# Differential attention in two halves of four heads, woven with weight tiles

## The chip, the cores and the metric

The kernel runs on one core of a Trainium2 chip, as one program. The metric is its time on the device in microseconds (us), of whole executions.

## The reference

Three layers follow each other on a sequence of 256 tokens with 1024 channels: retention with a PEER feed-forward, differential attention with a PEER feed-forward, and a last block (SwiGLU, RWKV-7 beside forgetting attention, SwiGLU). Everything is float32. The change is in the second one's attention. `k_sh` and `v_sh` are products of that stage's input with `kv_w`, the keys rotated; there are 8 heads, each with two maps of 64 dimensions and a value of 128.

```python
def diff_attention(x, w_q, lam_p, subln_g, w_out, k_sh, v_sh, layer_idx, angles):
    q = (x @ w_q).reshape(b, s, DIFF_HEADS, 2, DIFF_HEAD_DIM)
    q = rope(q, angles) * (DIFF_HEAD_DIM ** -0.5)
    lam = jnp.exp(jnp.sum(lp[0] * lp[1])) - jnp.exp(jnp.sum(lp[2] * lp[3])) + lam_init
    for i in range(s // Q_BLOCK):                       # blocks of 128 queries
        sc = jnp.einsum('bqhmd,bkhmd->bhmqk', qb, kb)   # keys up to the block's end
        p = jax.nn.softmax(jnp.where(mask, sc, -jnp.inf), axis=-1)
        a = p[:, :, 0] - lam * p[:, :, 1]
        outs.append(jnp.einsum('bhqk,bkhe->bqhe', a, vb))
    o = o * lax.rsqrt(jnp.mean(jnp.square(o), axis=-1, keepdims=True) + LN_EPS)
    o = o * subln_g * (1.0 - lam_init)
    return o.reshape(b, s, DIFF_HEADS * DIFF_V_DIM) @ w_out
```

`rope` turns the first 16 of the 64 dimensions. A layer norm of the residual sum follows.

## The kernel before

**Weights.** All weight matrices are cut into tiles of 128x1024 float32 (512 KB). `weight_tiles` (L52) lists them in the order of use; SyncE loads them in that order into a ring of four buffers. A matmul is made of three: each tile is split into a rounded part `hi` (ScalarE, L859) and the remainder `lo` = tile - `hi`, by VectorE (L1226) where the list says "V", by GpSimd (L1828) where it says "P". Activations are split likewise, and the three products of the larger parts are summed in PSUM. There are three `hi` and three `lo` buffers. The function `split(i)` of each engine works through the list up to tile i and is called with the number of the tile in use + 2, so a tile's parts are made up to two tiles ahead; ScalarE's `hi` waits until TensorE has finished the tile three places back, VectorE's and GpSimd's `lo` waits for that `hi`. SyncE reloads a ring buffer once the `lo` part is done.

**Order.** Every engine runs a program of its own, written out in Python as a sequence of operations in order, with waits on counters of the other engines. Where several strands of work share an engine, each is a generator and `weave` (L374) takes one step of each in turn, in the same order on all engines; one turn over all strands is called a round here.

**Differential attention** (`diff` in all four programs; TensorE from L555, ScalarE from L969, VectorE from L1446). TensorE transposes the input (`parts`, L400), and computes q, k and v in six groups: two groups (columns 0 to 511 and 512 to 1023) for each of the three matrices, a group being four tiles and two PSUM banks (`mat_n`, L428, matmuls in L441 to L443). ScalarE copies each group into `D_nat` (L979). VectorE rotates q and k in 24 small operations after all projections, four times six; TensorE waits for the last and transposes both (32 transposes, L405), and VectorE and ScalarE copy the results.

Then four strands `heads(tt, h0)` are woven, one for each block of 128 queries (`tt`; 128 keys for tt = 0, "narrow", and 256 for tt = 1, "wide") and each half of the heads (h0 = 0 or 4). For each of its four heads a strand has two score matmuls, one after the other (L578, L581); VectorE's mask and maximum (in `softmax_in`, then a scale by -0.125); ScalarE's two exponentials with sums (L966); VectorE's combination of both maps (`diff_a`: reciprocal, times lambda, two multiply passes); TensorE's transpose (L589); ScalarE's copy of it (L995); the product with the values (L596). After four heads ScalarE copies the bank of outputs to `D_o` (L999). VectorE makes the sums of squares of all heads, GpSimd the power -1/2 (`power`, L1835), VectorE two multiplies for each block (by that, and by `subln_g` times a constant). TensorE transposes the result (16 transposes) and multiplies by `w_out` in eight tiles (`mat_out`, L449, L469 to L471), each of which adds into four PSUM banks. VectorE's layer norm closes the stage. All VectorE operations but `lo` go through one helper at L1203, the transposed splits of `parts` on ScalarE through L868 (or L871 with a gain).

PSUM has eight banks; `bank(..., among=...)` takes them in turn from a given set and waits until the former holder is emptied. In `diff` before, projections use all eight, the score and transpose tiles of a strand one bank, its outputs another.

Two things lie beside it on GpSimd's queue: the loads of the lambda and `subln_g` rows at the start, and the load of the next layer norm's gains (`gains`, after the last projection).

Of the kernel before, what the change touches and what calls it, by code (L numbers as in the profile page):

```python
# [21 lines left out]
LN_EPS = 1e-5  # L22
# [10 lines left out]
for _name, _w in (("ffn1", 8), ("mix", 8), ("ffn2", 8), ("mu", 14), ("w0", 4), ("a0", 4), ("kk", 4),  # L33
                  ("ka", 4), ("rk", 4), ("lg", 4), ("lb", 4), ("fb", 1)):
    COLS[_name] = _n
    _n += _w
# [15 lines left out]
def weight_tiles():  # L52
# [23 lines left out]
    for name in ("diff_q", "kv_k", "kv_v", "diff_out"):  # L76
        for i in range(8):
            add(name, i)
# [66 lines left out]
def program(nc, A, out):  # L145
    ctx = ExitStack()
    with ctx:
# [129 lines left out]
        D_lamt, D_lp, D_ls, D_sub = a_(256), a_(128), a_(8), a_(128)  # L277
        D_nat = [a_(2048).rearrange("p (a d) -> p a d", a=2) for _ in range(3)]
        D_r = [a_(128).rearrange("p (h d) -> p h d", h=16) for _ in range(4)]
# [4 lines left out]
        for tt in range(2):  # L284
            for h0 in (0, 4):
                D_hd[tt, h0] = (a_(512).rearrange("p (m k) -> p m k", m=2), a_(512).rearrange("p (m k) -> p m k", m=2),
                                a_(256), a_(256), a_(2), a_(4))
        D_rr = a_(16).rearrange("p (a h) -> p a h", a=2)
# [97 lines left out]
        def tensor_program(pe):  # L386
# [168 lines left out]
            def diff():  # L555
                pe.wait_ge(*at(dve, "norm", 0, 1))
                parts("diff", lambda tt, c: tok3(x, tt, c), 8)
                for z in range(3):
                    for nb in range(2):
                        for _ in mat_n([TILE[D_names[z], nb * 4 + j] for j in range(4)], "diff", "diff_p", z, nb,  # L560
                                       first=z + nb == 0):
                            pass
                pe.wait_ge(*at(dve, "diff_rope"))
                parts("diff_q", lambda tt, c: tok3(D_nat[0], tt, c), 8)
                parts("diff_k", lambda tt, c: tok3(D_nat[1], tt, c), 8)
                for z in ("diff_q", "diff_k"):
                    for c in (4, 6):
                        pe.wait_ge(*(at(dve, z, "Tn", c) if c == 4 else at(act, z, "Tn", c)))

                def heads(tt, h0):  # L570
                    s, p, a2, aT, mx, ss = D_hd[tt, h0]
                    own = (tt * 2 + h0 // 4,)
                    for _ in range(tt):
                        yield
                    kw = 128 * (tt + 1)
                    for h in range(h0, h0 + 4):
# [8 lines left out]
                        yield  # L585
# [6 lines left out]
                        if h == h0:  # L592
                            ob = bank("diff_o", tt, h0, among=(4 + tt * 2 + h0 // 4,))
                        pe.wait_ge(*at(act, "diff_aT", tt, h))
                        for kb in range(tt + 1):
                            ins = pe.matmul(ob[:, (h % 4) * 128:(h % 4) * 128 + 128], aT[:, kb * 128:kb * 128 + 128],  # L596
                                            D_nat[2][:, kb, h * 128:h * 128 + 128], start=kb == 0, stop=kb == tt)
                        mm.done(ins, "diff_av", tt, h)

                weave([heads(tt, h0) for tt in range(2) for h0 in (0, 4)])  # L600
                pe.wait_ge(*at(dve, "diff_norm"))
                parts("diff_oT", lambda tt, c: tok3(D_o, tt, c), 8)
                mat_out("diff_out", [TILE["diff_out", i] for i in range(8)], lambda k: D_oT[:, k, :],
                        lambda k: [at(dve, "diff_oT", "Tl", k)] if k % 2 == 0 else [])
# [239 lines left out]
        def scalar_program(a):  # L844
# [18 lines left out]
            def parts(stage, nchunk, dst, gain=None):  # L863
                for c in range(0, nchunk, 2):
# [1253 lines left out]
```

## Time and profile before

| | us |
|---|---|
| median of three runs | 3005.3 (3004.41 to 3005.68) |
| the profiled execution | 3003.82 |
| its span, first to last instruction | 3001.8 |
| TensorE matmul busy | 2782.4 (93%) |
| VectorE busy | 1894.4 (63%) |
| ScalarE busy | 1239.1 (41%) |
| GpSimd busy | 770.4 (26%) |
| mean granted TensorE clock | 0.949 |

The profile is of one execution; its span leaves out 2.0 us around the first and last instruction. Engines are named PE (TensorE matmuls), PEld (its weight loads), DVE (VectorE), ACT (ScalarE), POOL (GpSimd). The tiles of this stage lie in one large area, so most of them appear under the name W. A float32 matmul of the heads appears as two records, a transpose as one. PEclk is the share of 2.4 GHz that TensorE was granted: 1.00 is 2.4 GHz, 0.50 is 1.2 GHz, and a value between them is a mixture in time. In a timeline, times are from the span's start, and a bracket says how long the engine was idle before and on whom it waited.

### The profile page before, as it was taken

The numbers are of one execution on the slowest core, as the hardware profiler recorded it, in microseconds if no ns is written. First come the engines' busy times: TensorE is split into PE (matmuls) and PEld (weight loads), VectorE is DVE, ScalarE is ACT, GpSimd is POOL, SyncE is SP. The second block draws the span as 40 slices with busy tenths as digits, with TensorE's granted clock in tenths as the row PEclk, the third lists the DMA queues.
The fourth block names the chain that finished last, engine by engine and source line by source line (L and its number), as shares of the span: only waits on it lengthen the run. The fifth ranks groups of instructions, "written<-read, shape, count | busy, mean of one in ns | idle before, by whom it ended". The sixth has DMA issues, their size and how long they took to land.

```text
span 3001.8 us, 43611 instructions
## 1 busy us (share of the span) xinstructions
PE 2782.4 (93%) x17592; PEld 2512.5 (84%) x17592; DVE 1894.4 (63%) x3246; ACT 1239.1 (41%) x1691; POOL 770.4 (26%) x336
## 2 busy tenths in 40 slices
PE   8989999999999988699999999999799858898998
PEld 7869999998888866499999988888798746776896
DVE  5655997776555556659977765555654675415554
ACT  4434463333545434244633345445444512132443
POOL 0001986664000000019876630000000230042000
PEclk9999999999999997699999999999899878889999
DMA  5454554445656643145544456656455410023554
GB/s 203 162 176 155 175 181 144 141 141 163 193 192 190 192 153 106 57 155 174 178 155 141 141 169 190 193 192 190 135 183 192 127 59 23 1 84 99 157 184 144
DMA packets 122919, 449.55 MB, mean 150 GB/s; under 512 B 13728, under 2 KB 13856, under 8 KB 122592
## 3 DMA queue, kind: packets, MB, share of 16 engines
q1 hardware_dynamic: 120800, 439.47, 45.9%
q0 software_dynamic: 1920, 7.30, 0.8%
q8 instruction: 140, 2.29, 0.3%
q14 instruction: 59, 0.48, 0.1%
HBM read 445.67 MB, written 1.05 MB: 149 GB/s over the span
## 4 chain that ended last, share of the span: by engine, by line
PE 84%; DVE 12%; ACT 2%; POOL 2%; issue 1%; DMA 0%; DVEq 0%; SPq 0%; ACTq 0%
PE ps L419 11%; PE ps L420 11%; PE ps L421 11%; PE ps L471 10%; PE ps L470 10%; PE ps L469 10%; DVE W L1203 9%; PE ps L538 4%; PE ps L623 3%; PE ps L441 2%; PE ps L442 2%; PE ps L443 2%; DVE x L1203 1%; PE ps L405 1%; POOL lo L1828 1%
## 5 line engine op out<-in xcount | busy, mean ns | idle before, releaser
L859 ACT ACTIVATE hi<-ring 128x1024 fp32r<-128x1024 f32 x830 | 878.5, 1059 | 1273.8 <-PE ps L421 649.8
L1226 DVE TENSOR_TENSOR lo<-ring,hi 128x1024 fp32r<-128x1024 f32 x544 | 665.7, 1225 | 604.2 <-ACT hi L859 604.0
L419 PE MATMUL ps<-xT_r,hi 128*128 128x256 f32 x3248 | 935.5, 288 | 11.7 <-POOL lo L1828 8.1
L420 PE MATMUL ps<-xT_r,hi 128*128 128x256 f32 x3248 | 921.1, 284 | 0.0
L421 PE MATMUL ps<-xT_r,lo 128*128 128x256 f32 x3248 | 920.8, 283 | 0.0
L1828 POOL TENSOR_TENSOR lo<-ring,hi 128x1024 fp32r<-128x1024 f32 x286 | 724.3, 2540 | 595.5 <-ACT hi L859 595.5
L419 PEld LDWEIGHTS ps<-xT_r,hi 128*128 128x128 f32 x3248 | 625.2, 192 | 15.6 <-POOL lo L1828 5.5
L420 PEld LDWEIGHTS ps<-xT_r,hi 128*128 128x128 f32 x3248 | 625.8, 193 | 0.7 <-issue 0.7
L421 PEld LDWEIGHTS ps<-xT_r,lo 128*128 128x128 f32 x3248 | 625.2, 192 | 0.0
L469 PE MATMUL ps<-hi,oht_r 128*128 128x512 f32 x1040 | 405.6, 390 | 13.6 <-DVE W L1203 13.6
L471 PE MATMUL ps<-hi,oht_r 128*128 128x512 f32 x1040 | 411.3, 395 | 0.0
L470 PE MATMUL ps<-lo,oht_r 128*128 128x512 f32 x1040 | 409.2, 393 | 0.0
L1835 POOL TENSOR_TENSOR small<-small,con 128x2 f32<-128x2 f32 (+2 forms) x16 | 16.3, 1018 | 1103.6 <-DVE small L1203 1103.6
L1203 DVE TENSOR_TENSOR W<-W,ps 128x512 f32<-128x512 f32 x240 | 164.6, 686 | 204.3 <-PE ps L538 119.5
L469 PEld LDWEIGHTS ps<-hi,oht_r 128*128 128x128 f32 x1040 | 196.2, 189 | 57.9 <-DVE W L1203 14.0
L470 PEld LDWEIGHTS ps<-lo,oht_r 128*128 128x128 f32 x1040 | 196.2, 189 | 45.9
L471 PEld LDWEIGHTS ps<-hi,oht_r 128*128 128x128 f32 x1040 | 196.4, 189 | 39.3
L1400 DVE TENSOR_SCALAR oht<-ps,selT 128x128 f32<-128x128 f32 x512 | 174.2, 404 | 0.0
L441 PE MATMUL ps<-hi,xT_r 128*128 128x512 f32 x336 | 138.9, 413 | 9.6 <-POOL lo L1828 6.0
L1203 DVE TENSOR_TENSOR W<-W 128x512 f32<-128x512 f32 (+6 forms) x127 | 128.1, 1009 | 16.4 <-ACT W L1043 7.5
L538 PE MATMUL ps<-oht 128*128 128x128 f32 x1024 | 134.6, 274 | 0.0
L442 PE MATMUL ps<-lo,xT_r 128*128 128x512 f32 x336 | 134.0, 399 | 0.0
(212 smaller groups left out, 2906.1 us busy)
## 6 DMA issues: line engine op xcount, KB each, us to landing
ring<-in_peer_u SPq DMA_DIRECT2D x256, 512.0 KB, 3.5
ring<-in_peer_v SPq DMA_DIRECT2D x256, 512.0 KB, 3.4
ring<-in_f SPq DMA_DIRECT2D x132, 512.0 KB, 3.6
ring<-in_ret_vg SPq DMA_DIRECT2D x32, 512.0 KB, 3.5
ring<-in_peer_q SPq DMA_DIRECT2D x32, 512.0 KB, 3.6
ring<-in_ret_qk SPq DMA_DIRECT2D x16, 512.0 KB, 3.8
ring<-in_ret_out SPq DMA_DIRECT2D x16, 512.0 KB, 4.1
ring<-in_in_shift SPq DMA_DIRECT2D x14, 512.0 KB, 4.1
```

The costliest lines, as they stand in the source:

```text
L419: pe.matmul(o, h, xT[:, k, 0:256], start=k == 0, stop=False)
L420: pe.matmul(o, h, xT[:, k, 256:512], start=False, stop=False)
L421: ins = pe.matmul(o, l, xT[:, k, 0:256], start=False, stop=k == 7)
L441: pe.matmul(bs[tt], xh, h, start=kk == 0, stop=False)
L469: pe.matmul(b, ah, h, start=k == 0, stop=False)
L470: pe.matmul(b, ah, l, start=False, stop=False)
L471: ins = pe.matmul(b, al, h, start=False, stop=k == len(tiles) - 1)
L538: ins = pe.matmul(b[:, s * 128:s * 128 + 128], hot[:, s, 1, :], hot[:, s, 0, :], start=True, stop=True)
L859: hid.done(a.activation(hi[m % NH][:, :], ring[j % NR][:, :], ACT.Copy), j)
L1203: dve.done(fn(*args), *name)
L1226: lo_v.done(v.tensor_tensor(lo[m % NH][:, :], ring[j % NR][:, :], as32(hi[m % NH][:, :]), ALU.subtract), j)
L1828: lo_p.done(p.tensor_tensor(lo[m % NH][:, :], ring[j % NR][:, :], as32(hi[m % NH][:, :]), ALU.subtract), j)
```

## The change

It rewrites `diff` in the four programs.

- **Halves.** All work goes in two halves of four heads (`nb` = 0, 1). The weight list takes the q, k and v tiles of heads 0 to 3 first, then those of heads 4 to 7. Of the second half's q and k tiles the odd ones are given to GpSimd ("P") for the `lo` part.
- **Rotation** is done per matrix and half (`rope(z, nb)`, six operations on both blocks at once), each called among the splits of later tiles.
- **First weave.** After three groups (12 tiles) and the transposes of q and k of heads 0 to 3, the heads of half 0 are woven with the 8 tiles of q and k of half 1: a strand `tiles_b`, first in the order, with one tile in each round, and four strands `heads(0, tt, u)` of two heads each, which start 0, 1, 1 and 2 rounds late. A head takes three rounds: scores (mask, maximum, exponentials), combination and transpose, product and output.
- **Between** come two value tiles and the transposes of q and k of half 1.
- **Second weave.** The heads of half 1 are woven with `tiles_c`: the norm of half 0 (VectorE only), two value tiles, the transposes of half 0's output, and four tiles of the output product.
- **After it** come the norm and transposes of half 1 (inside `mat_out_steps`, ahead of tile 4) and the last four output tiles.
- **Norm.** For every head and block ScalarE copies the 128x128 output and also squares it with a sum (`Square`, `accum_out`), so VectorE's squares and sums go; the sums of each half get their own power on GpSimd, and VectorE multiplies once per block by power and constant. `subln_g` becomes a column of per-partition gains applied in the two parts of the transposed output (`parts` with a gain), instead of a loaded row and a multiply.
- **Banks.** Projections and output product use banks 4 to 7; each strand's scores, transposes and outputs share one bank of 0 to 3.

The diff, cut to its core (`parts` and `natural` get an argument `first`; gains are passed as a function; ScalarE's `heads` follows the same steps):

```diff
-    for name in ("diff_q", "kv_k", "kv_v", "diff_out"):
-        for i in range(8):
-            add(name, i)
+    for half in range(2):
+        for name in ("diff_q", "kv_k", "kv_v"):
+            for i in range(half * 4, half * 4 + 4):
+                add(name, i, "P" if half and i % 2 and name != "kv_v" else "V")
+    for i in range(8):
+        add("diff_out", i)
...
+                def heads(nb, tt, u):          (TensorE)
+                    own = (tt * 2 + u,)
+                    for _ in range(tt + u):
+                        yield
...
+                    for h in range(nb * 4 + u * 2, nb * 4 + u * 2 + 2):
                         b = bank("diff_s", tt, h, among=own)
...
                         mm.done(ins, "diff_s", tt, h)
                         yield
-                        yield
                         b = bank("diff_t", tt, h, among=own)
                         pe.wait_ge(*at(dve, "diff_a", tt, h))
...
                         yield
+                        ob = bank("diff_o", tt, h, among=own)
                         pe.wait_ge(*at(act, "diff_aT", tt, h))
...
+                        yield
+                def out_ahead(k):
+                    if k == 4:
+                        pe.wait_ge(*at(dve, "diff_norm", 1))
+                        parts("diff_oT", lambda tt, c: tok3(D_o, tt, c), 8, among=LO4, first=4)
+                for z in range(3):
+                    for _ in group(z, 0):
+                        pass
+                turned(0, 0)
+                turned(1, 0)
+                def tiles_b():
+                    for z in range(2):
+                        yield from group(z, 1)
+                        yield
+                weave([tiles_b()] + [heads(0, tt, u) for u in range(2) for tt in range(2)])
+                values = group(2, 1)
+                next(values)
+                turned(0, 1)
+                next(values)
+                turned(1, 1)
+                output = mat_out_steps("diff_out", ..., among=HI4, ahead=out_ahead)
+                def tiles_c():
+                    yield from values
+                    yield
+                    pe.wait_ge(*at(dve, "diff_norm", 0))
+                    parts("diff_oT", lambda tt, c: tok3(D_o, tt, c), 4, among=HI4)
+                    yield
+                    for _ in range(4):
+                        next(output)
+                        yield
+                weave([tiles_c()] + [heads(1, tt, u) for u in range(2) for tt in range(2)])
+                for _ in output:
+                    pass
...
+                def group(z, nb):              (ScalarE)
+                    for j in range(4):
+                        split(TILE[D_names[z], nb * 4 + j] + 2)
+                        if j < 3:
+                            yield
+                    for tt in range(2):
+                        a.wait_ge(*at(mm, "diff_p", z, nb))
...
+                        a.wait_ge(*at(mm, "diff_av", tt, h))
+                        o = ps("diff_o", tt, h)[:, 0:128]
+                        act.done(a.activation(D_o[:, tt, h * 128:h * 128 + 128], o, ACT.Copy))
+                        act.done(a.activation(D_sq[...], o, ACT.Square, accum_out=D_rr[nb][...]), "diff_o", nb)
+                        empties(act, "diff_o", tt, h)
+                        yield
...
+                def rope(z, nb):               (VectorE)
+                    v.wait_ge(*at(act, "diff_p", z, nb, 1))
+                    tt_(r[0], x1, dcos, ALU.mult)
...
+                def norm(nb):
+                    v.wait_ge(*at(act, "diff_o", nb))
+                    rsqrt(D_rr[nb], D_rr[nb], 1.0 / 128, LN_EPS, "diff", nb)
+                    for tt in range(2):
+                        stt_(ov, ov, 1.0 - LAM_INIT, b3(D_rr[nb][...], [128, 4, 128], 2), ALU.mult, ALU.mult, name=("diff_norm", nb))
+                def tiles_b():
+                    for z in range(2):
+                        for j in range(4):
+                            tiles(z, 1, (j,))
+                            if z == 1 and j == 1:
+                                rope(0, 1)
+                            yield
...
+                tiles(2, 1, (0,))
+                rope(1, 1)
+                tiles(2, 1, (1,))
+                natural("diff_q", 8, D_qT, first=4)
+                natural("diff_k", 8, D_kT, first=4)
+                def tiles_c():
+                    norm(0)
+                    for j in range(2, 4):
+                        tiles(2, 1, (j,))
+                        yield
+                    parts("diff_oT", 4, D_oT, lambda c: pc("dsub"))
+                    yield
+                    for i in range(4):
+                        split(TILE["diff_out", i] + 2)
+                        yield
...
-            load("diff", [(D_lamt, prow(12, 256)), (D_sub, prow(11, 128))], [at(dve, "norm", 0, 1)])
+            load("diff", [(D_lamt, prow(11, 256))], [at(dve, "norm", 0, 1)])
+            split(TILE["kv_k", 7])             (GpSimd)
+            power(D_rr[0], "diff", 0)
             gains(1, 0, mm, "diff_p", 2, 1)
-            power(D_rr, "diff")
+            power(D_rr[1], "diff", 1)
```

## Rows read from the trace of the kernel before

**Rows 1.** The page's chain that ended last, by engine

```profile
PE 84%; DVE 12%; ACT 2%; POOL 2%; issue 1%; DMA 0%; DVEq 0%; SPq 0%; ACTq 0%
```

**Rows 2.** Windows of the differential-attention stage (first line: columns)

```profile
core 0: us, PE busy (x) PEld busy (x) DVE busy (x) ACT busy (x) POOL busy (x), PEclk, DMA share, GB/s
1092.50:1155.10 62.60, 62.60 (x276) 51.77 (x276) 30.18 (x29) 31.12 (x36) 0.00 (x0) 1.00 0.58 182
1155.10:1165.50 10.40, 2.94 (x14) 2.09 (x13) 8.15 (x25) 2.15 (x3) 1.06 (x2) 0.79 0.68 219
1165.50:1172.70 7.20, 6.53 (x32) 6.29 (x32) 2.77 (x4) 2.39 (x4) 0.00 (x0) 0.60 0.01 2
1172.70:1227.20 54.50, 48.75 (x136) 28.95 (x136) 39.93 (x114) 21.31 (x84) 0.00 (x0) 0.52 0.00 1
1227.20:1238.70 11.50, 0.04 (x1) 0.04 (x1) 7.56 (x8) 0.58 (x1) 2.93 (x1) 0.50 0.00 0
1238.70:1242.30 3.60, 3.60 (x17) 3.60 (x18) 1.53 (x3) 1.79 (x3) 0.00 (x0) 0.50 0.00 0
1242.30:1264.70 22.40, 22.40 (x97) 17.98 (x95) 11.04 (x10) 8.95 (x9) 0.00 (x0) 0.98 0.53 164
```

**Rows 3.** Timeline 1155 to 1173: start us, length us, engine, line, operation

```profile
1155.40 1.06 ACT L859 ACTIVATE hi<-ring 128x1024 fp32r<-128x1024 f32 x1 [1.66 <-PE ps L443]
...
1156.50 1.23 DVE L1226 TENSOR_TENSOR lo<-ring,hi 128x1024 fp32r<-128x1024 f32 x1 [1.49 <-ACT hi L859]
...
1165.48 6.54 PE L405 MATMUL ps<-con,W 128*128 128x128 f32 x32 [7.46 <-DVE W L1203]
...
1172.92 0.46 PE L578 MATMUL ps<-W 64*128 64x128 f32 x2 [0.89 <-ACT W L877]
```

**Rows 4.** Timeline of the heads, 1180 to 1192, blocks of 256 keys

```profile
1180.32 0.51 ACT L966 ACTIVATE W<-W 128x256 f32<-128x256 f32 x1 [0.85 <-DVE W L1203]
...
1181.23 0.18 ACT L966 ACTIVATION_READ_ACCUMULATOR W<-W 128x1 f32 x1
...
1183.48 0.17 DVE L1203 RECIPROCAL W<-W 128x2 f32<-128x2 f32 x1
...
1183.87 0.36 DVE L1203 TENSOR_SCALAR W<-W 128x256 f32<-128x256 f32 x1
...
1184.26 0.48 DVE L1203 SCALAR_TENSOR_TENSOR W<-W 128x256 f32<-128x256 f32 x1
...
1184.90 0.66 PE L589 MATMUL ps<-con,W 128*128 128x128 f32 x2 [0.71 <-DVE W L1203]
...
1191.19 1.22 PE L581 MATMUL ps<-W 64*128 64x256 f32 x2
```

**Rows 5.** Groups by form, heads: count | busy us, mean ns | idle

```profile
L1203 DVE TENSOR_TENSOR W<-ps,con 128x512 f32<-128x512 f32 x8 | 5.5, 692 | 5.4 <-PE ps L581 4.8
...
L1203 DVE TENSOR_TENSOR W<-ps,con 128x256 f32<-128x256 f32 x8 | 3.4, 425 | 2.4 <-PE ps L578 1.6
```

**Rows 6.** Timeline of the mixer, 2465 to 2475

```profile
2465.93 0.69 DVE L1203 TENSOR_TENSOR W<-W,small 128x512 f32<-128x512 f32 x1 [1.75 <-POOL small L1835]
...
2471.62 5.11 POOL L1828 TENSOR_TENSOR lo<-ring,hi 128x1024 fp32r<-128x1024 f32 x2
2471.69 2.81 DVE L1203 TENSOR_TENSOR W<-W,small 128x512 f32<-128x512 f32 x1 [1.75 <-POOL small L1835]
...
2474.02 0.79 PE L441 MATMUL ps<-hi,xT_r 128*128 128x512 f32 x1 [4.50 <-POOL lo L1828]
...
2474.61 0.63 PE L442 MATMUL ps<-lo,xT_r 128*128 128x512 f32 x1
```

**Rows 7.** Groups by form, whole run

```profile
L1203 DVE SCALAR_TENSOR_TENSOR xT_r<-ps,col,xT_r 128x256 fp32r<-128x256 f32 x24 | 11.6, 484 | 7.6 <-ACT xT_r L871 6.2
...
L884 ACT ACTIVATE W<-x 128x512 f32<-128x512 f32 x16 | 10.1, 630 | 24.3 <-DVE x L1203 24.1
...
L1835 POOL TENSOR_TENSOR small<-small,con 128x8 f32<-128x8 f32 x4 | 6.6, 1653 | 31.3 <-DVE small L1203 31.3
```

More of the change, by code:

```diff
@@ new lines, in diff @@
+                weave([tiles_b()] + [heads(0, tt, u) for u in range(2) for tt in range(2)])
[4 more added lines that the diff above has]
+                turned(1, 1)
+                output = mat_out_steps("diff_out", [TILE["diff_out", i] for i in range(8)], lambda k: D_oT[:, k, :],
+                                       lambda k: [at(dve, "diff_oT", "Tl", k)] if k % 2 == 0 else [], among=HI4, ahead=out_ahead)
@@ L860, in split, with parts @@
                     todo[0] += 1
-            def parts(stage, nchunk, dst, gain=None):
-                for c in range(0, nchunk, 2):
+            def parts(stage, nchunk, dst, gain=None, first=0):
+                for c in range(first, nchunk, 2):
                     pv = j2(ps(stage, "T", c))
@@ L870, in parts, with natural @@
                         for j in range(2):
-                            act.done(a.activation(dst[:, c + j, 0:256], pv[:, j, :], ACT.Identity, scale=pc(gain, c + j)),
+                            act.done(a.activation(dst[:, c + j, 0:256], pv[:, j, :], ACT.Identity, scale=gain(c + j)),
                                      stage, "Th", c)
-            def natural(stage, nchunk, dst):
-                for c in range(2, nchunk, 4):
+            def natural(stage, nchunk, dst, first=0):
+                for c in range(first + 2, nchunk, 4):
                     a.wait_ge(*at(mm, stage, "T", c))
@@ L1227, in split, with parts @@
                     todo[0] += 1
-            def parts(stage, nchunk, dst, gain=None):
-                for c in range(0, nchunk, 2):
+            def parts(stage, nchunk, dst, gain=None, first=0):
+                for c in range(first, nchunk, 2):
                     pv = j2(ps(stage, "T", c))
@@ L1512, in diff @@
+                weave([tiles_c()] + [heads(1, tt, u) for u in range(2) for tt in range(2)])
+                norm(1)
+                parts("diff_oT", 8, D_oT, lambda c: pc("dsub"), first=4)
+                for i in range(4, 8):
                     split(TILE["diff_out", i] + 2)
@@ L1543, in mixer @@
                 rms("mix", M_xs)
-                parts("mix", 8, xT, "mix")
+                parts("mix", 8, xT, lambda c: pc("mix", c))
                 for i in range(2):
```

202 lines of the change are left out of this document (100 added, 102 removed).

## The prediction

> **What bounds the kernel now.** I read the chain of waits first: TensorE holds 84% of it and VectorE 12% [rows 1]. A change pays where TensorE stands still or runs slowly, so next I cut the differential-attention stage at TensorE's own stops and asked for busy time and granted clock by stretch [rows 2]. From the first projection matmul (1092.5) to the last one of the output product (1264.7) it takes 172.2 us. Six projection groups: 24 tiles in 62.6 us, 2.61 us a tile, TensorE always busy, clock 1.00. Rotation: 10.4 us, of which 7.5 us idle [rows 2, 3]. Transposes of q and k: 7.2 us. Heads: 54.5 us, TensorE busy 48.7 us of them, but at 0.52: almost all at the 1.2 GHz level. Norm and its transposes: 11.5 + 3.6 us. Output: 22.4 us. The DMA share is 0.58 at most while tiles run, so loads bound nothing here.
>
> **The change, part by part.** All other stages keep their instructions. The sum is a new length for the 172.2 us.
>
> *First three groups.* 12 tiles x 2.61 = 31.3 us. Rotation of q and k now runs in VectorE's slack under later tiles. Work for one tile is a `hi` part of 1.06 us and a `lo` part of 1.23 us [rows 3], begun two tiles (5.2 us) before use, so 2.9 us are free; one rotation is six operations of 0.3 us, 1.9 us (a quarter of the 24 in the 7.9 us before the transposes). Hidden: 0. Were this cover gone, each of the four would cost 1.9 us.
>
> *Transposes of the first half of q and k.* 16, where 32 took 6.6 us [rows 3]: 3.3 us at the low clock, half of it at the high one. I take 2.7. The copies behind them lie under the first woven tile.
>
> *The two weaves.* This decides. Engines work in order, and in each round of a weave every engine's tile step stands ahead of its four head steps. ScalarE cannot begin the next `hi` before the last exponential of the round; VectorE cannot take the next head step before `lo`, which waits for that `hi`; TensorE waits for VectorE's combination `diff_a` before it transposes, and its next scores stand behind that transpose. So a round is a loop through three engines, not the busiest engine's sum. Its links, for a wide head (256 keys): combination 1.25 us (from the reciprocal's start at 1183.48 to 1184.74); exponentials 1.1 (0.51 to the end of the second read, 1180.32 to 1181.41); score pair 2 x 1.22 = 2.4 at the low clock [rows 4], 1.2 at the high one, since the narrow pair began there at 0.46 [rows 3]; mask and maximum 0.69 each, scale 0.17 (as the reciprocal's), with gaps 1.6 [rows 4, 5]. Narrow (128 keys), from 0.43 for the mask [rows 5] and scaled likewise: 1.1, 0.9, 1.0, 1.05. Transpose with its hops 0.45 to 0.6; copy of the transposed block 0.4; output copy plus squares 0.6.
> Rounds 2 and 5 (transpose, transpose, wide score): 1.1 + 1.25 + 1.25 + 1.1 + 0.45 + 1.2 + 1.6 + 1.1 = 9.05. Rounds 1 and 4 (a narrow transpose, then both scores): 1.1 + 1.25 + 1.1 + 0.45 + 1.2 + 1.6 + 1.05 + 0.9 = 8.65. Round 3: 1.1 + 1.25 + 1.05 + 2.1 (an exponential, two outputs) + 0.4 = 5.9. Round 6: 1.1 + 1.25 + 1.25 + 0.6 = 4.2. Where GpSimd makes the `lo` part (rounds 1, 3 and 5 of the first weave), `hi` and `lo` leave the loop: minus 2.35; in round 3 TensorE's tile and score then hold it, plus 0.8; round 5 carries a rotation, plus 1.9.
> First weave: start 5.6 (tile, score, mask, exponential) + 6.3 + 9.05 + 4.35 + 8.65 + 8.6 + 4.2 + last round 3.2 = 50.0 us. Second: start 7.9, for the first half's norm sits ahead of the mask (0.2 + 1.65 for the power [rows 7] + 2 x 0.75), + 8.65 + 8.9 (output transposes' two parts, 2.2, in place of `hi` and `lo`) + 5.9 + 8.65 + 9.05 + 4.2 + 1.0 = 54.3 us.
>
> *Clock in the weaves.* Before, the heads never left the low level though TensorE was 90% busy [rows 2]. Here a round has one tile and stops of up to 5 us. After a stop of 4.50 us the mixer's tile restarts with two matmuls 0.59 us apart, where twelve share 2.61 us [rows 6]: the low level. A slow tile is mostly hidden in the loop's wait; slow scores are not. All low: four wide scores a weave x 1.2, plus the tile ahead of round 3's score, 13 us in both. All high: 0. Between ends this far apart I take the middle, 6.5, since a round is half dense tile and half short work.
>
> *GpSimd's four tiles.* In the mixer a 128x512 VectorE operation with both inputs in SBUF took 0.69 us alone and 2.81 us when it began just behind a GpSimd split [rows 6]: 2.1 us lost. Four splits: 0 to 8.4 us; two of them fall on combinations, so I take 3. The Trainium skill (SBUF — State Buffer, "Who interferes with whom") has the rule: a VectorE instruction with two SBUF inputs contends with a GpSimd instruction that reads SBUF, and the loser waits for the whole instruction. It speaks against this part; by it every split would lose its 2.1 us to some operation of VectorE and the sum be 5.4 us longer, 177.9; the trace agrees that the loss is the rest of the split.
>
> *Between the weaves.* Two tiles and 16 transposes, 5.2 + 2.0 = 7.2 us; the last rotation ends 6 us into it and is just hidden.
>
> *Tail.* Output copy and squares 0.8, scale 0.2, power 1.65, two multiplies 1.4, four transposes 0.9 (3.6 for 16), their two parts 1.7 (VectorE's 0.48 a chunk [rows 7], ScalarE's about the same, overlapped): 6.7 us, where 15.1 stood. Then four output tiles, 10.8 us.
>
> *Edits at nothing.* ScalarE's squares: a 128x512 one is 0.63 us [rows 7], the 128-wide one lies between 0.2 and 0.6; 16 of them are in the rounds above, and cost up to 0.3 us each if ScalarE ends the loop. Gain per chunk in the transposed copies: same count of stages, two instructions for one, 0.4 us in all. The load of the gain row goes from GpSimd's queue, which was idle. In that queue the four splits and the first half's power now stand ahead of the next norm's gains, needed only at the layer norm, 12 tiles later. SyncE's order of loads changes, not its number: a slot is reloaded when its `lo` is done, and at the 182 GB/s of the projections [rows 2] a tile of 512 KB comes in 2.9 us, less than any round.
>
> Sum: 31.3 + 2.7 + 50.0 + 7.2 + 54.3 + 6.7 + 10.8 = 163.0, plus 3 (port), plus 6.5 (clock) = 172.5 us against 172.2. The profiled execution took 3003.8 us (span 3001.8 and 2.0 around it), 1.5 below the median 3005.3; a difference carries over, so I forecast 3005.5. Ends: 163.0 gives 2996, 163.0 + 13 + 8.4 = 184.4 gives 3017.5. Said otherwise: the gaps give 21 us (rotation 10.4, transposes 2.5, tail 8.4) and the weaves give it back: with port and clock 114 us, for heads and 14 tiles that took 54.5 + 36.7.
>
> **Rivals.** *A, the engines run ahead of each other.* The weaves then cost TensorE's own work: 14 tiles 36.7, transposes 1, heads 48.7 us halved by the clock with some left over, 27; 65 us, with today's stretch (54.5/48.7) 72. Stage 131, time 2964. For it: neither ScalarE nor VectorE has much over 30 us of work in a weave by the links above (VectorE's heads 4 x (1.6 + 1.25 + 1.05 + 1.1) = 20, `lo` parts 5 to 7.4, rotation or norm 2). Against: the order of steps above, which leaves each only one round of slack. Halfway, 2984.
>
> *B, slower by the clock.* Stops of 4 to 5 us in rounds 2 and 5 drop TensorE to 1.2 GHz for most of both weaves; scores double and a tile of 5.1 us no longer fits under rounds 3 and 6. It decides once over two thirds of the weaves run low: the other 6.5 us of the clock term give 3012, and some 2.3 us for the tile in each of four rounds 3021. For it: the stretch from 1172.7 on; against: rounds of 4 us without a long stop.
>
> *C, the rotation is not hidden* (a barrier elsewhere): up to 7.6 us back, inside the range. The change cannot fail to act: the order of all five streams is written out.
>
> **How the numbers follow.** About 0.2% (6 us) is what a measurement of this kernel can tell from no change. The loop with mixed clock: 0.52, 2996 to 3017.5, of which faster 0.12, same 0.27, slower 0.13. A or part of it: 0.24, faster. B: 0.22, slower. C: 0.02, same. Faster 0.36, same 0.29, slower 0.35. The range takes A's half-way point and most of B: 2982 to 3021.
>
> **What would show it.** Right: no TensorE stop before the transposes of q and k; weaves of 50 to 60 us each with waits of TensorE on VectorE of 3 to 5 us before the head transposes, and of `lo` on `hi` on exponentials; clock there 0.6 to 0.9; a tail of 6 to 8 us; DMA idle. Wrong: weaves of 35 to 40 us (A), clock near 0.50 in them (B), or VectorE's combinations unchanged beside GpSimd's splits (no port term).

## The result, and the profile after

| | before | changed |
|---|---|---|
| median of 16 runs, us | 3004.8 (3002.8 to 3010.1) | 3013.4 (3010.9 to 3018.5) |
| span of the profiled execution, us | 3001.8 | 3011.6 |
| from the first projection matmul to the last of the output product, us | 172.2 | 179.2 |
| mean granted TensorE clock | 0.949 | 0.953 |

The changed kernel takes 1.0028 times the time of before, 95% interval 1.0020 to 1.0036: 8.4 us slower, a little more than the 6 us that were called the limit of no change. Of the 9.8 us between the two spans 7.0 lie in this stage, 0.9 before it and 1.9 behind it.

The windows of the changed kernel's stage, in the columns of [rows 2] (length; busy us and count of PE, PEld, DVE, ACT, POOL; PEclk; DMA share; GB/s). In order: first three groups, first transposes of q and k, first weave, between, second weave, tail, last four output tiles.

```profile
1093.40:1127.30 33.90, 33.90 (x146) 27.90 (x146) 18.68 (x29) 16.64 (x19) 1.50 (x1) 0.97 0.54 169
1127.30:1129.00 1.70, 1.70 (x17) 1.70 (x16) 1.07 (x2) 1.58 (x3) 0.88 (x1) 1.00 0.09 34
1129.00:1186.40 57.40, 45.38 (x166) 31.67 (x165) 28.57 (x68) 23.23 (x73) 7.05 (x3) 0.79 0.23 74
1186.40:1193.70 7.30, 7.30 (x42) 6.19 (x41) 4.81 (x10) 3.61 (x8) 0.00 (x0) 1.00 0.46 144
1193.70:1252.75 59.05, 40.87 (x148) 27.68 (x147) 29.66 (x70) 22.28 (x74) 2.81 (x3) 0.77 0.25 80
1252.75:1259.96 7.21, 1.97 (x10) 1.60 (x9) 2.57 (x6) 2.54 (x8) 1.66 (x1) 0.74 0.00 1
1259.96:1272.60 12.64, 12.64 (x48) 9.97 (x48) 5.73 (x6) 3.79 (x4) 0.00 (x0) 0.88 0.39 126
```

The stop before the transposes of q and k is gone, and the tail is 7.2 us where [rows 2] has 11.5 + 3.6. The time came back in the two weaves: 57.4 and 59.1 us, in which no engine is full. VectorE is busy for half of them, ScalarE for 40%, and TensorE stands still for 12 us of the first and 18 us of the second. Round 2 of the first weave shows why; this is its timeline (start us, length us, engine, line, operation, idle before and releaser):

```profile
1141.26 0.19 ACT L1005 ACTIVATION_READ_ACCUMULATOR W<-W 128x1 f32 x1
1141.35 1.04 ACT L898 ACTIVATE hi<-ring 128x1024 fp32r<-128x1024 f32 x1
...
1142.43 1.23 DVE L1294 TENSOR_TENSOR lo<-ring,hi 128x1024 fp32r<-128x1024 f32 x1 [1.89 <-ACT hi L898]
...
1143.57 0.16 DVE L1271 RECIPROCAL W<-W 128x2 f32<-128x2 f32 x1
...
1143.96 0.35 DVE L1271 TENSOR_SCALAR W<-W 128x256 f32<-128x256 f32 x1
1144.35 0.48 DVE L1271 SCALAR_TENSOR_TENSOR W<-W 128x256 f32<-128x256 f32 x1
...
1144.97 0.66 PE L594 MATMUL ps<-con,W 128*128 128x128 f32 x2 [3.52 <-DVE W L1271]
```

The last exponential's sum is read; only then comes `hi`, only then `lo`, only then the combination, and TensorE has stood still for 3.5 us. The chain of waits goes through such a `hi` behind the exponentials five times in the two weaves (at 1141.4, 1179.1, 1200.8, 1237.0 and 1247.5). Behind the stops it goes through a score pair and then through TensorE's tile at the low clock: the tile from 1149.0 to 1154.2 took 5.2 us. The waits of both weaves (1129 to 1253; engine, line, whom it waited for: us in total, times, longest):

```profile
ACT W L1005 <- DVE W L1271: 38.6, 12, 4.7
...
PE ps L594 <- DVE W L1271: 28.6, 15, 5.0
DVE W L1271 <- PE ps L587: 26.2, 11, 4.5
ACT W L1032 <- PE ps L594: 24.5, 16, 3.5
...
DVE lo L1294 <- ACT hi L898: 22.5, 11, 2.7
```

Exponentials wait for the maximum, transposes for the combination, masks for the scores, copies for the transposes: a ring of waits.

### The profile page after: what moved, and what is told of

It reads as the page before. It is cut to its first block, busy times and chain, and to the rows that moved or that the text cites. A ratio compares the mean times of both kernels' runs of the same rounds, so it can differ in the third digit from the quotient of the medians.

```text
span 3011.6 us, 43694 instructions
## 1 busy us (share of the span) xinstructions
PE 2782.8 (92%) x17592; PEld 2511.7 (83%) x17592; DVE 1884.4 (63%) x3243; ACT 1244.5 (41%) x1739; POOL 778.7 (26%) x340
## 4 chain that ended last, share of the span: by engine, by line
PE 82%; DVE 13%; ACT 2%; POOL 2%; issue 1%; DMA 0%; DVEq 0%; SPq 0%; ACTq 0%
PE ps L423 11%; PE ps L424 11%; PE ps L425 11%; PE ps L473 10%; PE ps L475 10%; PE ps L474 10%; DVE W L1271 10%; PE ps L542 4%; PE ps L662 3%; PE ps L445 2%; PE ps L446 2%; PE ps L447 2%; DVE x L1271 1%; POOL lo L1929 1%; PE ps L409 1%
## 5 line engine op out<-in xcount | busy, mean ns | idle before, releaser
L1929 POOL TENSOR_TENSOR lo<-ring,hi 128x1024 fp32r<-128x1024 f32 x290 | 732.8, 2534 | 669.8 <-ACT hi L898 669.8
L445 PE MATMUL ps<-hi,xT_r 128*128 128x512 f32 x336 | 142.5, 424 | 9.2 <-POOL lo L1929 5.5
L447 PE MATMUL ps<-hi,xT_r 128*128 128x512 f32 x336 | 136.3, 406 | 0.0
```

Source lines behind the costliest of these rows:

```text
L445: pe.matmul(bs[tt], xh, h, start=kk == 0, stop=False)
L1929: lo_p.done(p.tensor_tensor(lo[m % NH][:, :], ring[j % NR][:, :], as32(hi[m % NH][:, :]), ALU.subtract), j)
```

## The experiments

Each run has its own runs of the kernel before on the same chip; microseconds of a difference between two experiments are taken from their ratios, times 3004. By the intervals of the ratios such a difference is known to 4 to 5 us either way.

The whole time also holds the other stages, which no edit touches, and they did not always take the same time. So the length of this stage in each run's profiled execution is given beside it, as "stage": from the end of the input's transposes to the last matmul of the output product, 172.2 us before and 179.2 changed. What lies behind the stage took 1737.1 us before and 1739.0 in the changed kernel, but only 1730.3, 1729.8 and 1730.2 in three of the runs below (`lo` behind the head steps, the fourth corner, and the same head order inside the weaves). More than half of that difference lies in one stretch of the last block, from the `hi` of one weight tile to that of the next. Here it is in the changed kernel and then in these three:

```profile
2489.20:2653.60 164.40, 137.14 (x781) 119.04 (x780) 72.78 (x123) 35.22 (x79) 2.40 (x1) 0.79 0.02 7
2470.20:2629.40 159.20, 131.27 (x780) 113.59 (x779) 73.61 (x124) 35.12 (x78) 2.55 (x1) 0.82 0.02 8
2471.10:2630.10 159.00, 131.81 (x780) 113.99 (x779) 73.65 (x124) 35.09 (x78) 2.67 (x1) 0.81 0.03 8
2455.30:2614.50 159.20, 131.27 (x780) 113.61 (x779) 73.55 (x124) 35.12 (x78) 2.55 (x1) 0.82 0.02 7
```

The same matmuls were busy for 131 to 132 us instead of 137, at a granted clock of 0.81 or 0.82 instead of 0.79. It is not the chip: two other runs on the chip of the first of the three, those without GpSimd and with the rotation alone, took 1738.8 and 1737.5 us behind the stage. The reason is not shown. So up to 9 us of the gain of these three runs did not come about in this stage.

**VectorE's `lo` behind the head steps.** In VectorE's program alone:

```diff
-                weave([tiles_b()] + [heads(0, tt, u) for u in range(2) for tt in range(2)])
+                weave([heads(0, tt, u) for u in range(2) for tt in range(2)] + [tiles_b()])
...
-                weave([tiles_c()] + [heads(1, tt, u) for u in range(2) for tt in range(2)])
+                weave([norm_c()] + [heads(1, tt, u) for u in range(2) for tt in range(2)] + [tiles_c()])
```

`norm_c` holds the norm of half 0 and the parts of its transposes, in their old rounds.

> The changed kernel with one edit: in both weaves VectorE takes its tile step (the lo part) after the four head steps of a round instead of ahead of them; the half's norm and the parts of the output transposes stay first. The same instructions on every engine. Loop theory: in the eight rounds in which VectorE makes a lo part, lo (1.23 us) and the wait for hi (1.1 us) leave the chain from exponential to combination: 14 to 19 us less than the changed kernel, 2994 to 2999 us, so also 6 to 11 below the kernel before; each weave 47 to 52 us instead of 57.4 and 59.1. Rival (the weaves are long because TensorE's clock is low and its own work is slow): less than 4 us gained, 3009 to 3013.

Measured: 2990.3 us, ratio 0.9958 (0.9944 to 0.9972). That is 0.0070, or 21 us, below the changed kernel, and 13 us below the kernel before. Not one instruction was added or taken away. The stage took 164.1 us, 15.1 less than in the changed kernel, which is within the 14 to 19 us that the loop theory asked for; 8.7 of the 24 us between the two profiled executions lie behind the stage. Its weaves:

```profile
1128.70:1179.10 50.40, 41.41 (x168) 29.56 (x167) 29.60 (x68) 23.05 (x74) 7.06 (x3) 0.90 0.27 83
1186.10:1236.30 50.20, 36.98 (x151) 25.53 (x149) 29.53 (x71) 22.08 (x74) 2.81 (x3) 0.86 0.27 85
```

16 us come out of the weaves (57.4 + 59.1 to 50.4 + 50.2). TensorE stands still for 22 us of them instead of 30, and the clock is 0.90 and 0.86. How much of the gain is the clock's is not shown.

**GpSimd's four tiles given back to VectorE.**

```diff
-                add(name, i, "P" if half and i % 2 and name != "kv_v" else "V")
+                add(name, i)
```

> The changed kernel with the four tiles that GpSimd splits given back to VectorE. Loop theory: lo and the wait for hi come back into the chain of three rounds of the first weave, plus 7 us, less the one operation that the trace shows held by GpSimd (2.25 us where 0.35 is usual, minus 1.9): 3 to 6 us slower than the changed kernel, 3016 to 3019. Rival (the shared port is what makes the first weave long, 2.1 us for each tile): 3 to 8 us faster, 3005 to 3010.

Measured: 3018.2 us, ratio 1.0055 (1.0041 to 1.0068), 8 us slower than the changed kernel; stage 184.5, 5.3 longer. The rival is out: handing tiles to GpSimd helps here, as the loop theory says, by taking `lo` out of VectorE's order.

**No weave of tiles with heads.**

```diff
-                weave([tiles_b()] + [heads(0, tt, u) for u in range(2) for tt in range(2)])
+                weave([tiles_b()])
+                weave([heads(0, tt, u) for u in range(2) for tt in range(2)])
```

and so for the second, on all three engines.

> The changed kernel with its two weaves undone: on every engine the tile strand runs to its end and then the four head strands are woven with each other. Halves, rotation per half, ScalarE's squares and the short tail stay. Loop theory (the weave costs more than it covers): first stretch 8 tiles 21.8 + heads 27 + 3 to start and drain = 52 instead of 57.4, second 16.4 + 3 + 27 + 3 = 49 instead of 59.1: 12 to 18 us faster than the changed kernel, 2995 to 3001. Rival (the weave does cover tiles with heads, and the loss is elsewhere, in halves or squares): 0 to 20 us slower, 3013 to 3033.

Measured: 3015.3 us, ratio 1.0042 (1.0029 to 1.0056). A miss: undoing the weave gained nothing. By the whole time it cost 4 us, no more than the intervals allow for chance; the stage took 187.0 us, 7.8 more than in the changed kernel. A half of the heads alone takes 38.5 us and not 27 + 3:

```profile
1150.00:1188.50 38.50, 23.12 (x70) 13.65 (x70) 18.75 (x56) 14.55 (x63) 0.00 (x0) 0.57 0.06 21
1221.50:1260.30 38.80, 23.09 (x69) 13.39 (x68) 18.76 (x56) 13.47 (x62) 0.00 (x0) 0.57 0.05 14
```

TensorE is busy for only 23 of the 38.5 us, where [rows 2] has 48.7 of 54.5 for all eight heads. The price of the heads had been taken from an order that the changed kernel no longer has.

**The rotation alone.** Kernel before; in VectorE's loop over the tiles:

```diff
                         for j in range(4):
                             split(TILE[D_names[z], nb * 4 + j] + 2)
+                            if z and nb == 0 and j % 2:
+                                rope(z - 1, j // 2)
```

> The kernel before with one edit: each of the four rotations (a matrix and a block of 128 queries) is called among the splits of later tiles, after every second tile of the group that follows, instead of after all projections. Theory: TensorE's stop of 7.5 us before the transposes of q and k goes and nothing else moves: 2997 to 2998. Rival (a rotation of 1.9 us makes lo parts late and TensorE waits): 3000 to 3005.

Measured: 2995.3 us, ratio 0.9971 (0.9960 to 0.9981), 8.7 us faster; stage 161.9, 10.3 shorter. The stop of 7.5 us between the last tile and the transposes is gone and no tile is late: the 24 tiles took 65.5 us at clock 1.00. The transposes follow them at once at clock 1.00 and took 3.6 us, where [rows 2] has 7.2 us at 0.60.

**Filler matmuls, for the clock.** Changed kernel; the extra matmuls change no result:

```diff
                         b = bank("diff_t", tt, h, among=own)
+                        if tt == 1 and u == 0:
+                            for k in range(8):
+                                pe.matmul(b, xT[:, 4, 0:128], xT[:, 4 + k % 4, :], start=True, stop=True)
                         pe.wait_ge(*at(dve, "diff_a", tt, h))
```

> The changed kernel with eight dense 128x512 matmuls of no use (their bank is overwritten by the transpose that follows) ahead of TensorE's wait for the combination of the first wide strand, where the trace shows stops of 3.5 to 5.4 us: four places. Nothing is left out of the computation. Theory that the low clock costs some microseconds of the weaves: granted clock of the rounds around these stops goes from 0.64 to 0.70 up to over 0.9, the wide score pair behind each from 2.5 to 1.3 us and the tile behind it from 4.6 to 2.9, partly hidden: 4 to 8 us faster than the changed kernel, 3005 to 3009. Rival (the loop through VectorE and ScalarE hides TensorE's clock): 3012 to 3015.

Measured: 3006.5 us, ratio 1.0009 (1.0000 to 1.0017): 5.7 us below the changed kernel, by 32 matmuls of no use. Windows of the changed kernel (score pair behind the stop of round 2, then its tile), and of both weaves with filler:

```profile
1146.10:1149.02 2.92, 2.81 (x6) 1.25 (x6) 0.00 (x0) 0.28 (x1) 0.00 (x0) 0.50 0.08 32
1149.02:1153.60 4.58, 4.58 (x12) 3.61 (x12) 1.55 (x3) 2.04 (x5) 0.78 (x1) 0.50 0.00 0
```

```profile
1128.80:1185.40 56.60, 48.38 (x184) 34.55 (x182) 28.80 (x68) 23.28 (x74) 7.07 (x3) 0.85 0.24 75
1192.40:1251.80 59.40, 46.10 (x167) 31.90 (x164) 29.78 (x71) 22.17 (x74) 2.81 (x3) 0.80 0.24 80
```

The clock rises only from 0.79 and 0.77 to 0.85 and 0.80. Behind the first stop the first of the two wide score products took 0.7 us instead of 1.2, but the tile behind them took 5.5 us (1148.3 to 1153.8) where it had taken 5.2, and 2.9 had been expected. The two weaves took 116.0 us instead of 116.5 and the stage 178.7 instead of 179.2. The profiled execution, 3013.3 us, was the slowest of eleven (from 3003.8), so it may not be the typical one. So what the low clock cost in the weaves is not settled: the medians say 5.7 us (give or take 3.5), the trace shows 0.5.

**The parts of the transposes later,** on top of the first experiment: behind the head steps on VectorE, one round later on ScalarE, output tiles one round later.

```diff
                     for j in range(2, 4):
                         tiles(2, 1, (j,))
                         yield
+                    parts("diff_oT", 4, D_oT, lambda c: pc("dsub"))
+                    yield
                     yield
```

> The kernel of the run e1_lo_last with one edit in the second weave: both parts of the four output transposes come after the head steps of their round on VectorE and at the head of the next round on ScalarE, and the output tiles begin one round later, so that the last of them lies beside the last strand. Theory: the stop of 6.4 us that this round still has shrinks to 2 to 3 us: 3 to 5 us faster than e1_lo_last, 2985 to 2988. Rival (it only moves the wait to the first output tile): 2989 to 2992.

Measured: 2994.3 us, ratio 0.9963 (0.9950 to 0.9976), not to be told from 0.9958; stage 164.8 against 164.1. The rival held: the stop of 6.4 us became one of 2.9 and one of 6.0 before the next transposes, because VectorE's parts now stood ahead of the next combination and waited for ScalarE.

**Four strands of four heads, with the new norm.** The rotation run plus ScalarE's copy and square for each head, power for each block, one multiply, gain in the parts. No halves, no weave with tiles.

```diff
+                        a.wait_ge(*at(mm, "diff_av", tt, h))
+                        o = ps("diff_o", tt, h)[:, 0:128]
+                        act.done(a.activation(D_o[:, tt, h * 128:h * 128 + 128], o, ACT.Copy))
+                        act.done(a.activation(D_sq[...], o, ACT.Square, accum_out=D_rr[tt][:, h:h + 1]), "diff_o", tt)
```

> The kernel of the run e4_rotation_only (four strands of four heads, no halves, no weave with tiles) with the norm of the changed kernel: ScalarE copies and squares each head's output, GpSimd's power per block of queries, one multiply, gain in the parts of the transposes. Theory: VectorE's squares and one of two multiplies leave the stop of 11.5 us before the output transposes, minus 5 us; the 16 squares lie in ScalarE's idle time: 2989 to 2992. Rival (ScalarE's extra 0.6 us a head delays the exponentials of the next): 2995 to 3000.

Measured: 2989.1 us, ratio 0.9948 (0.9935 to 0.9961): 7 us below the rotation run; stage 154.5, 7.4 shorter. The squares cost next to nothing here, where ScalarE has idle time: the heads took 55.4 us instead of 55.1.

**The same with the head weave cut in two.**

```diff
-                weave([heads(tt, h0) for tt in range(2) for h0 in (0, 4)])
+                for half in range(2):
+                    weave([heads(tt, h0, half) for tt in range(2) for h0 in (0, 4)])
```

> The kernel of the run e7_no_halves with the weave of the heads cut in two: each strand's first two heads, then each strand's last two. The changed kernel without its weaves takes 38.5 us for a half of the heads by its trace, where the kernel before takes 54.5 for all eight. Theory (a half costs a fill and a drain of the strands): 5 to 9 us slower than e7_no_halves. Rival (the changed kernel's order inside a head, scores, combination and output in successive rounds with each strand one round late, is what costs): 0 to 4 us slower.

Measured: 2988.1 us, ratio 0.9943 (0.9930 to 0.9956); stage 154.4, heads 55.3 us. Cutting the head weave in two costs nothing, at least where the halves follow each other directly. So the theory I had put first is out. What is left is the order of the heads' steps and the banks: a strand of the changed kernel has one, a strand here two.

**The stagger alone** (starts and order of the four strands), in the kernel without weaves:

```diff
-                    for _ in range(tt + u):
+                    for _ in range(tt):
...
-                weave([heads(0, tt, u) for u in range(2) for tt in range(2)])
+                weave([heads(0, tt, u) for tt in range(2) for u in range(2)])
```

> The kernel of the run e3_no_weave with one edit: the four head strands start 0, 0, 1 and 1 rounds late, in the order narrow, narrow, wide, wide, as in the kernel before, instead of 0, 1, 1 and 2. If the stagger is what makes a half of the heads take 38.5 us there: 10 to 16 us faster than e3_no_weave, 2999 to 3005. If it is the step order inside a head (scores and transpose in successive rounds, with VectorE and ScalarE between them in one round): 0 to 6 us faster, 3009 to 3015. I expect the second.

Measured: 3003.0 us, ratio 0.9999 (0.9990 to 1.0008): 13 us below the kernel without weaves; stage 175.5, 11.5 shorter. I had expected the other outcome. The half of the heads takes 34.0 us instead of 38.5.

**Stagger and pause, without weaves.** In addition one more `yield` between a head's scores and its transpose on TensorE, and ahead of mask and exponentials on the others:

```diff
                         mm.done(ins, "diff_s", tt, h)
                         yield
+                        yield
                         b = bank("diff_t", tt, h, among=own)
```

> The kernel of the run e3_no_weave with both edits of e10_order_woven in its head strands (pause between scores and transpose, starts 0, 0, 1, 1), tiles and heads still one after the other. Theory (the order inside a head is the loss of the changed kernel without its weaves): a half of the heads takes 27 to 31 us instead of 38.5, TensorE without stops at the low clock: 14 to 22 us faster than e3_no_weave, 2993 to 3001. Rival (halves, banks or ScalarE's extra operations): less than 8 us faster, 3007 or more.

Measured: 2998.7 us, ratio 0.9984 (0.9975 to 0.9993): 17 us below the kernel without weaves, 4.5 of it by the pause; stage 168.8, 18.2 shorter, 6.7 of it by the pause. A half takes 30.0 us with the banks of the changed kernel, so the banks are no large part of the 38.5:

```profile
1149.30:1179.30 30.00, 19.54 (x70) 12.57 (x70) 18.73 (x56) 14.60 (x63) 0.00 (x0) 0.59 0.08 24
```

**The same head order inside the weaves,** with `lo` behind the head steps:

> The kernel of the run e1_lo_last with the head order of the kernel before in its weaves: a round's pause between a head's scores and its transpose on all engines, so that mask, maximum, exponentials and combination have a round more, and starts 0, 0, 1, 1. Theory (what is left in the weaves is the chain scores, mask, exponential, combination, transpose inside neighbouring rounds): TensorE's stops in the weaves shrink from some 16 us to under 6 and its clock rises: 8 to 18 us faster than e1_lo_last, 2972 to 2982. Rival (nine rounds for eight and the fuller queues take it back): 2986 to 2994.

Measured: 2979.4 us, ratio 0.9924 (0.9911 to 0.9937). It beats every other version: 23 us below the kernel before, 31 below the changed one, with the same instructions as the changed one. Its stage took 150.3 us, 28.9 less than in the changed kernel. Its weaves and their waits:

```profile
1127.50:1169.70 42.20, 36.06 (x167) 26.75 (x166) 32.32 (x68) 23.16 (x75) 7.25 (x3) 0.96 0.32 102
1178.30:1221.40 43.10, 34.67 (x150) 24.97 (x148) 29.65 (x71) 21.88 (x74) 2.81 (x3) 0.87 0.34 110
```

```profile
PE ps L595 <- DVE W L1273: 13.2, 7, 4.0
DVE lo L1296 <- ACT hi L899: 10.5, 6, 2.9
```

TensorE waits for the combination for 13 us instead of 29, and the weaves take 85 us instead of 116. The theory had asked for stops under 6 us in all, so that part of it was missed. Of what is left, one wait of 2.8 us is GpSimd's:

```profile
1143.98 2.48 POOL L1937 TENSOR_TENSOR lo<-ring,hi 128x1024 fp32r<-128x1024 f32 x1 [9.88 <-ACT hi L899]
1144.29 2.44 DVE L1273 SCALAR_TENSOR_TENSOR W<-W 128x256 f32<-128x256 f32 x1
...
1146.88 0.41 PE L595 MATMUL ps<-con,W 128*128 128x128 f32 x2 [2.81 <-DVE W L1273]
```

**The fourth corner:** the new head order with `lo` still ahead of the head steps.

> The changed kernel (VectorE's tile step ahead of the head steps) with the head order of the kernel before in its weaves, as in e10_order_woven: the fourth corner of the square of lo first or last and old or new order. Theory (hi and lo ahead of the head steps bind every round: exponential, hi 1.1, lo 1.25, two combinations 2.5, two masks 2.1, exponential 0.9 is some 7 us a round, 9 rounds a weave, less the ends): 5 to 15 us faster than the changed kernel, 2998 to 3008. Rival (the order alone frees the loop, and lo ahead costs little then): within 5 us of e10_order_woven, 2976 to 2985.

Measured: 2990.9 us, ratio 0.9957 (0.9943 to 0.9971), between what the two theories asked for. Its stage took 166.0 us, 13.2 less than in the changed kernel, which is inside the first theory's 5 to 15. The square, as ratios to the kernel before and length of the stage:

| | `lo` ahead of the head steps | `lo` behind them |
|---|---|---|
| scores and transpose in successive rounds, starts 0, 1, 1, 2 | 1.0028, 179.2 us (the changed kernel) | 0.9958, 164.1 us |
| a round between them, starts 0, 0, 1, 1 | 0.9957, 166.0 us | 0.9924, 150.3 us |

By the whole time each edit alone takes 21 us off and both together 31, as if the second were worth less once the first is made. The stage shows no such thing: 15.1 and 13.2 us alone, 28.9 together. Most of the difference is the 8.7 to 9.2 us behind the stage, which each of the three profiled executions has once. In the stage the two edits add up, as far as one profiled execution of each can tell. (That of the best version, 2974.9 us, was the fastest of six, the slowest 2987.5.)

## Why the prediction was right, and where its steps failed

The forecast was 3005.5 us with 2982 to 3021 around it; 3013.4 is inside, on the slower side. The side was not called: faster had 0.36 and slower 0.35, and of the 0.35 most was rival B, which did not come. The mechanism that did come, the loop, had 0.13 for slower. The range is wide, 39 us, and part of the closeness is luck: the 6.5 us for the clock were the middle between 0 and 13, chosen without a row for it, and the weaves came out within 2.7 us of the sum with it. Point by point:

- **The loop** (rounds bound by a chain through three engines): right. The trace has it link by link, moving `lo` alone took 15 us out of the stage, and the weaves were 57.4 and 59.1 us where the terms say 50.0 + 3 + 3.25 = 56.2 and 54.3 + 3.25 = 57.6 (port and half the clock term each time as they were charged). Measured on ScalarE, from the last exponential of a round to that of the next, rounds 1 to 5 of the first weave took 6.7, 10.4, 5.4, 10.5 and 11.5 us, where the terms without clock and port say 6.3, 9.05, 4.35, 8.65 and 8.6. Rival A fell with it.
- **The tile of 2.61 us**: mis-sized. The window ended at 1155.1, the last step of the chain of waits there, but matmuls ran until 1158.0. The right cut reads

```profile
1092.50:1158.00 65.50, 65.50 (x288) 53.85 (x287) 31.64 (x32) 32.18 (x37) 0.00 (x0) 1.00 0.58 183
1158.00:1165.50 7.50, 0.04 (x2) 0.02 (x1) 6.68 (x23) 1.08 (x2) 1.06 (x2) 0.71 0.69 221
```

  that is 288 matmuls, 2.73 us a tile. The 2.9 us of tile work had been counted as part of the rotation's 10.4, so the stop that the hidden rotation took away was 7.5 us, not 10.4. (The run with it alone has a stage 10.3 us shorter, because its transposes also ran at full clock.) The first groups took 33.9 us instead of 31.3; 1.4 of that is the tile's size, and the rest goes with the first matmuls, at the low clock until 1095.8. The same 12 tiles took 32.8 us in the profile of the fourth corner, so that part varies between executions.
- **Last four output tiles**: 12.6 us instead of 10.8. The first of them starts with matmuls of 0.77 and 0.63 us; the clock was low behind the tail's stop. The term had no price for it. Together with the item above, these are 4.4 of the 6.7 us by which the stage was longer than its sum of 172.5; the weaves have 2.7, tail and between 0.6, and the first transposes gave 1.0 back.
- **Tail** 7.2 for 6.7 and **between** 7.3 for 7.2: right. GpSimd's power of 128x8 took 1.66 us.
- **Clock**: the level was right, 0.79 and 0.77 in the asked 0.6 to 0.9. The term of 6.5 us is not settled: the filler run's medians say 5.7, its trace 0.5. One step under it was wrong: a slow tile was to be mostly hidden in the loop's wait, but the chain of waits runs through the tile at the low clock in round 3 (5.2 us). Rival B did not come: it was mostly the rounds behind long stops that ran low.
- **Port**: 3 us had been charged for four tiles. One operation was held, for 1.9 us (below). And the other side of the ledger, `lo` out of VectorE's order, was worth more: without GpSimd the kernel is 8 us slower and the stage 5.3 us longer.
- **"The gaps give 21 us and the weaves give it back"**: the sum nearly held (the gaps gave 7.5 by the rotation, 3.7 by the transposes and 7.9 by the tail, 19 us), and this reading of it did not. Cutting the weaves apart gave nothing back, because the heads alone had become slower too: 38.5 us a half against 27. The step that failed is the price of "54.5 us" as what heads cost outside a weave. What the gaps had gained was lost by two choices of order, worth 15 and 13 us of the stage: `lo` ahead of the head steps, and a head's scores, combination and transpose in neighbouring rounds with starts 0, 1, 1, 2. Neither the weave, nor the halves, nor the squares was the loss.

What stays open: which of stagger and pause counts inside a weave (they were parted only outside it); what the low clock cost in the weaves; how much of the 2.3 us by which a half (30.0 us) is still longer than half of the run with the head weave cut in two (27.7) is the banks' and how much the filling and draining of the strands; and why the stages behind this one took 1730 us in some profiled executions and 1739 in others. The best version's stage is only 4.1 us shorter than that of the run with the head weave cut in two (150.3 against 154.4), which needs no weaving with tiles.

## What to carry to other kernels

Where strands are woven by hand on engines that work in order, write down for one round the chain that goes through all of them (here exponential, `hi`, `lo`, combination, transpose, scores, mask, exponential): in this case its sum was the round's length within 3 us, though no engine was full. Put work that is needed two rounds later (`lo`) behind the steps that another engine waits for in this round, and try a round between a producer and its consumer. Price a part from the order in which it will run: a half of the heads took 30.0, 34.0 or 38.5 us by order alone. Where a change is worth a few microseconds of 3000, read the length of its own stage in the trace beside the whole time: here the stages that nobody had edited differed by up to 10 us between profiled executions.

## What the runs showed of the hardware that had not been expected

GpSimd's split held a VectorE operation with one tensor input. In the changed kernel, from the timeline of the first weave:

```profile
1169.15 2.34 POOL L1929 TENSOR_TENSOR lo<-ring,hi 128x1024 fp32r<-128x1024 f32 x1 [13.96 <-ACT hi L898]
...
1169.39 2.25 DVE L1271 TENSOR_SCALAR W<-W 128x256 f32<-128x256 f32 x1
...
1171.68 0.48 DVE L1271 SCALAR_TENSOR_TENSOR W<-W 128x256 f32<-128x256 f32 x1
```

The TENSOR_SCALAR takes 0.35 us elsewhere (1143.96 above); here it ended just behind GpSimd's instruction, as the two-input one did in [rows 6]. The prediction had counted only operations with two inputs in SBUF. The size of the held operation did not matter: in the fourth corner's trace a TENSOR_SCALAR of 128x2 took 1.74 us instead of 0.17 beside a split, and the TENSOR_REDUCE ahead of it, beside the same split, its usual 0.42. The Trainium skill (SBUF — State Buffer, "Who interferes with whom") says that `tensor_scalar` too can contend, in its 2-port modes; the trace agrees that it can be held, and does not show the mode.

In the best version the clock came back further than the 0.6 to 0.9 that the prediction gave for a weave. That the heads alone run at the low level was known from [rows 2]. In the run without halves, their stretch reads

```profile
1163.80:1213.00 49.20, 44.54 (x124) 26.04 (x124) 35.27 (x105) 23.69 (x111) 0.00 (x0) 0.53 0.04 15
```

TensorE is busy for 91% of the time with float32 scores, transposes and products of 128 and 256 columns, at 0.53. A half of the heads in the stagger-and-pause order ran at 0.59 without tiles (30.0 us) and at 0.96 with a tile of twelve 128x512 matmuls in nearly every round (first weave of the best version, 42.2 us); the second weave, where TensorE stood still for 8.4 of 43.1 us, had 0.87. In this kernel the tiles woven among the heads went with the high clock as long as the stops were short. These runs were not built to part the two.
